# One gated-MLP stage in seven block products with its side loads reordered, in a four-layer float32 kernel on one Trainium2 core

## What is computed

```python
def first_block(...):                       # DEPTH = 2 layers
    sc = silu(c)
    for layer in range(DEPTH):
        mod = sc @ w_mod[layer] + b_mod[layer]          # 1024 x 6144 weights for one row
        shift1, scale1, gate1, shift2, scale2, gate2 = split(mod, 6)
        h = rmsnorm(x, g_attn[layer]) * (1 + scale1) + shift1
        x = x + gate1 * mixer_layer(h, w_in[layer], w_out[layer], ...)
        h = rmsnorm(x, g_mlp[layer]) * (1 + scale2) + shift2
        up = h @ w_up[layer]                             # 1024 x 5632
        u, g = up[..., :D_FF], up[..., D_FF:]            # D_FF = 2816
        g = causal_depthwise_conv(g, conv_w[layer], conv_b[layer])   # 3 taps
        x = x + gate2 * ((silu(g) * u) @ w_down[layer])

def hybrid_layer(x, ...):                   # second block, 2 layers
    mixed = concat(rms_norm(out_a), rms_norm(out_b), rms_norm(out_c))
    x = x + mixed @ w_out
    x = x + expert_choice_moe(rms_norm(x, norm_ffn), w_router, ..., w_gate, w_up, w_down)
```

## Time and profile before

| what | value |
|---|---|
| median of 3 runs | 1944.18 us (1943.29 to 1944.21) |
| the profiled execution: its own time | 1942.48 us |
| the profiled execution: span of its instructions | 1940.7 us |
| TensorE busy | 1653.6 us, 85% of the span |
| VectorE / ScalarE / GpSimd busy | 710.2 / 285.6 / 142.3 us |
| mean granted TensorE clock | 0.937 of full speed |
| data moved | 599.75 MB, mean 309 GB/s |

### The profile page before, as it was taken

How to read it: one execution, slowest core, us unless ns; L and a number is a source line. 1 busy time by engine, 2 the same in 40 slices (tenths; PEclk the granted TensorE clock), 3 DMA queues, 4 the chain that set the end, 5 groups by cost and what they waited for, 6 DMA issues and landing times.

```text
span 1940.7 us, 24600 instructions
## 1 busy us (share of the span) xinstructions
PE 1653.6 (85%) x10484; PEld 943.2 (49%) x10484; DVE 710.2 (37%) x1482; ACT 285.6 (15%) x773; POOL 142.3 (7%) x149
## 2 busy tenths in 40 slices
PE   8999999999999999999786766757999785756757
PEld 3456988544579964474432232322474432232322
DVE  1583666977628976274010010101274110010101
ACT  1243000021511001253000010001253000010000
POOL 0011000000214510310000000000220000000000
PEclk9999999999999999999897987979999898987978
DMA  9992788755235643646999999999745999999998
GB/s 354 341 338 73 249 303 299 273 196 184 88 119 185 236 151 126 192 174 259 403 429 431 427 432 426 433 429 407 252 174 238 389 430 431 425 431 427 434 428 349
DMA packets 164164, 599.75 MB, mean 309 GB/s; under 512 B 18928, under 2 KB 78064, under 8 KB 140272
## 3 DMA queue, kind: packets, MB, share of 16 engines
q1 hardware_dynamic: 163838, 598.03, 78.4%
q10 hardware_dynamic: 242, 0.53, 0.1%
HBM read 594.75 MB, written 3.80 MB: 308 GB/s over the span
## 4 chain that ended last, share of the span: by engine, by line
PE 57%; DMA 38%; DVE 3%; ACT 1%; issue 1%; POOL 0%; SPq 0%; DVEq 0%; ACTq 0%
DMA extra<-in_w_down 14%; DMA extra<-in_w_up 12%; DMA extra<-in_w_gate 11%; PE ps L1266 9%; PE ps L1379 6%; PE ps L1332 6%; PE ps L1304 5%; PE ps L1619 5%; PE ps L949 4%; PE ps L1118 4%; PE ps L1517 3%; PE ps L1216 3%; PE ps L1639 1%; DMA ring<-in_w_mod 1%; PE ps L835 1%; PE ps L857 1%
## 5 line engine op out<-in xcount | busy, mean ns | idle before, releaser
L1619 PE MATMUL ps<-ring,wide 128*32 128x256 f32 x2912 | 217.9, 465 | 120.8 <-DMA ring<-in_w_up 76.2
L1619 PEld LDWEIGHTS ps<-ring,wide 128*32 128x32 f32 x2912 | 107.3, 133 | 225.3 <-DMA ring<-in_w_up 85.8
L1639 PE MATMUL ps<-ring,wide 128*32 128x512 f32 x768 | 158.7, 641 | 45.6 <-DMA ring<-in_w_down 41.9
L3204 DVE TENSOR_TENSOR wide<-ps,wide 128x512 f32<-128x512 f32 x16 | 10.7, 670 | 508.1 <-PE ps L1619 508.1
L1266 PE MATMUL ps<-hT,ring 128*128 128x256 f32 (+1 forms) x1088 | 183.8, 330 | 0.0
L1266 PEld LDWEIGHTS ps<-hT,ring 128*128 128x128 f32 x1088 | 166.6, 191 | 17.3 <-issue 2.9
L1619 PE MATMUL ps<-extra,wide 128*32 128x256 f32 x1056 | 89.9, 512 | 62.7 <-DMA extra<-in_w_up 40.3
L1379 PE MATMUL ps<-ring,hT 128*128 128x512 f32 (+2 forms) x320 | 127.3, 555 | 0.4 <-issue 0.4
L1639 PEld LDWEIGHTS ps<-ring,wide 128*32 128x32 f32 x768 | 44.7, 117 | 155.5 <-issue 122.4
L2375 DVE SCALAR_TENSOR_TENSOR extra<-ring,sc,extra 128x512 f32<-128x512 f32 x140 | 109.8, 784 | 5.2
L1619 PEld LDWEIGHTS ps<-extra,wide 128*32 128x32 f32 x1056 | 41.9, 146 | 109.5 <-DMA extra<-in_w_up 44.2
(11 more groups left out here) (372 smaller groups left out, 2102.6 us busy)
## 6 DMA issues: line engine op xcount, KB each, us to landing
ring<-in_w_gate SPq DMA_DIRECT2D x24, 4096.0 KB, 31.4
ring<-in_w_down SPq DMA_DIRECT2D x24, 4096.0 KB, 33.7
ring<-in_w_up SPq DMA_DIRECT2D x20, 4096.0 KB, 32.6
ring<-in_w_mod SPq DMA_DIRECT2D x24, 2048.0 KB, 12.9
ring<-in_w_up SPq DMA_DIRECT2D x44, 1024.0 KB, 8.0
extra<-in_w_gate SPq DMA_DIRECT2D x8, 4096.0 KB, 35.1
extra<-in_w_up SPq DMA_DIRECT2D x8, 4096.0 KB, 33.0
ring<-in_w_in SPq DMA_DIRECT2D x13, 2048.0 KB, 13.0
```

What stands on the lines that cost most here:

```text
L1619: last = mm(ps[2 * part + e // 2][j * CAP:(j + 1) * CAP, e % 2 * 2 * P:(e % 2 + 1) * 2 * P], xsT[:, k, e * CAP:(e + 1) * CAP], expert_row( ...
L1639: last = mm(ps[6 + n][e * CAP:(e + 1) * CAP, :], hidT[:, e, k, :], expert_row(n0, e, k)[:, n * N:(n + 1) * N], start=k == 0, stop=k == KD - 1)
```

## The change

It has five parts.

1. `UP_WHOLE` becomes `(5, 2)`: layer 0's up tiles 5 to 10 are made by `up_seven` too, with all that belongs to it on GpSimd, VectorE and ScalarE.
2. The late modulations of layer 0 are moved by four tables. `FOLD_AFTER` places the tiles in the list and the folds on TensorE: 10 and 11 after the output projection (TensorE makes them after the first half of up tile 1), 12 and 13 after up tile 1, 14 and 15 after up tile 2, 16 after 3, 17 and 18 after 4, 19 after 7, 20 after 9, 21 after down tile 2. `SUM_WHOLE`, `SUM_FIRST` and `SUM_PARTS` place the sums on VectorE. The sums use three buffers in turn instead of two.
3. The convolution's first tap moves from VectorE to ScalarE in both layers, and VectorE's order of convolution, joins and row sums around a seven-product tile is another.
4. The router of the second block: rows of `w_router` are laid out in blocks, so that the load has 64-byte runs instead of 512-byte ones; its weights are multiplied by `norm_ffn` once, on GpSimd; the flipped rows are then copied by one instruction of 512 columns on each of ScalarE and VectorE instead of four scaled ones of 128.
5. `mixed_squares` runs once per attention map over four maps instead of four times in a row.

```diff
-UP_WHOLE = (11, 2)
+UP_WHOLE = (5, 2)
+FOLD_AFTER = ({("out", 1): (10, 11), ("up", 1): (12, 13), ("up", 2): (14, 15), ("up", 3): (16,), ("up", 4): (17, 18),
+               ("up", 7): (19,), ("up", 9): (20,), ("down", 2): (21,)}, {("up", 6): (0,), ("up", 7): (1,)})
+SUM_WHOLE = {0: (14,), 1: (15,), 2: (16, 17), 3: (18,)}
...
-        tiles += [(l, "out", j) for j in range(2)]
-        late = MODS[l][EARLY[l]:]
-        steps = [(l, "up", j) for j in range(UPT)] + [(l, "down", j) for j in range(NDOWN)]
-        for n, t in enumerate(steps):
+        tiles.append((l, "out", 0))
+        for t in [(l, "out", 1)] + [(l, "up", j) for j in range(UPT)] + [(l, "down", j) for j in range(NDOWN)]:
             tiles.append(t)
-            if LAGS[l] <= n < len(late) + LAGS[l]:
-                tiles.append((late[n - LAGS[l]][0], "mod", late[n - LAGS[l]][1]))
+            tiles += [(MODS[l][q][0], "mod", MODS[l][q][1]) for q in FOLD_AFTER[l].get(t[1:], ())]
...
-                                 a["w_router_2"].rearrange("l (p k) n -> p l k n", k=KD)).then_inc(sems["router_loaded"], 16)
+                                 a["w_router_2"].rearrange("l (k p) n -> p l k n", k=KD)).then_inc(sems["router_loaded"], 16)
...
                 up(1, 0, P)
                 stream_ready(2 * L + 1, 1)
+                folds(("out", 1))
                 up(0, P, P)
                 up(1, P, P)
+                folds(("up", 1))
...
-                        if j > 2:
-                            pe.wait_ge(*up_read(s, m, j - 1))
+                        if j > first:
+                            pe.wait_ge(*up_read(s, L, m, j - 1))
+                        elif m == 6 and L == 0:
+                            pe.wait_ge(*s.at("b1_mod_ready", FOLD_AFTER[0][("up", first - 1)][-1] + 1))
                         elif m == 5:
-                            pe.wait_ge(*s.at("b1_product_ready", 2))
+                            pe.wait_ge(*s.at("b1_product_ready", first - first % 2))
+                        elif m == 3:
+                            pe.wait_ge(*s.at("b1_product_ready", first - 1 + first % 2))
...
-                    for f in range(2):
-                        ts(y[:, f, :], gp[:, f, :], cc1(L, "conv_w", 2 * FCH + 2 * j + f), cc1(L, "conv_b", 2 * j + f),
-                           ALU.mult, ALU.add).then_inc(s.up(), 1)
...
+                first = UP_WHOLE[L]
+                for j in range(first - 1):
+                    conv(j)
+                    up_gated(j)
+                    if L == 0:
+                        for q in SUM_WHOLE[j]:
+                            accumulate(q)
+                up_second(first)
+                up_rows_sums()
                 if L == 0:
-                    mod_out(EARLY[L] + UPT - LAGS[L])
+                    mod_out(17)
+                    mod_out(18)
+                for j in range(first, UPT):
+                    if j in SUM_FIRST[L]:
+                        accumulate(*SUM_FIRST[L][j])
+                    conv(j - 1)
+                    up_join(j, UP_READS[:1])
+                    up_fourth(j)
+                    up_gated(j - 1)
+                    if j in SUM_PARTS[L]:
+                        accumulate(*SUM_PARTS[L][j])
...
-                    for k in range(4, 8):
-                        ts(h8[:, k, c * P:(c + 1) * P], ps[5 - 4 * c][:, (k - 4) * P:(k - 3) * P],
-                           c2(L, "norm_ffn", k), None, ALU.mult).then_inc(s.up("b2_x_by_dve" if k == 7 else None), 1)
+                    cp(h8[:, 4 - 4 * c:8 - 4 * c, c * P:(c + 1) * P], ps[5 - 5 * c][:, :].rearrange("p (k t) -> p k t", k=4))\
+                        .then_inc(s.up("b2_x_by_dve"), 1)
```

More of the change, by code:

```diff
@@ L56 @@
 EARLY = (10, 0)
-LAGS = (2, 6)
 MOD_BANK = 2
@@ L124, with _up_acts @@
 TAB = {}
+def _up_acts(l):
+    first = UP_WHOLE[l]
+    acts = [(what, j) for j in range(first - 1) for what in ("tap", "silu")]
+    for j in range(first, UPT):
+        acts += [("tap", j - 1), ("copy", j), ("silu", j - 1)]
+    return acts + [("tap", UPT - 1), ("silu", UPT - 1)]
+UP_ACTS = [_up_acts(l) for l in range(DEPTH)]
+UP_SEVEN = [UPT - UP_WHOLE[l] for l in range(DEPTH)]
 def _tab():
@@ L899, in modulation @@
                     if i // 2 in (2, 5):
-                        last = mm(ps[b][:, :], ones, acc[:, q % 2, :], start=True, stop=True)
+                        last = mm(ps[b][:, :], ones, mod_sum(L, q), start=True, stop=True)
                     else:
                         for n in range(4):
-                            last = mm(ps[b][:, n:n + 1], acc[:, q % 2, n * P:(n + 1) * P], ones[:, 0:1],
+                            last = mm(ps[b][:, n:n + 1], mod_sum(L, q)[:, n * P:(n + 1) * P], ones[:, 0:1],
                                       start=True, stop=True)
@@ L1279, in _, with folds @@
                 stream_ready(2 * L + 1, 1)
+                def folds(step):
+                    for q in FOLD_AFTER[L].get(step, ()):
+                        modulation(q)
+                folds(("out", 1))
                 up(0, P, P)
                 up(1, P, P)
-                late = len(MODS[L]) - EARLY[L]
+                folds(("up", 1))
                 def up_seven(j):
-                    pe.wait_ge(*b1_loaded(B1_AT[(1, "up", j)]))
-                    w, h = up_weights(j), in_rows()
+                    first = UP_WHOLE[L]
+                    pe.wait_ge(*b1_loaded(B1_AT[(L, "up", j)]))
+                    w, h = up_weights(L, j), in_rows()
                     s1, s2 = up_scratch(j)
@@ L1317, in _ @@
                         up(j, 0, T)
-                    if 0 <= j - LAGS[L] < late:
-                        modulation(EARLY[L] + j - LAGS[L])
+                    folds(("up", j))
                 pe.wait_ge(*s.at("b1_product_ready", UPT - 1))
@@ L1349, in _ @@
                     last.then_inc(tile_done, 1)
-                    if UPT + j - LAGS[L] < late:
-                        modulation(EARLY[L] + UPT + j - LAGS[L])
+                    folds(("down", j))
                 for j in DOWN_TAIL:
@@ L1921, in _, with up_copies @@
                     av(pT[:, j % 2, :], sm[:, j % 2, :], ACT.Silu).then_inc(s.up("b1_up_by_act"), 1)
+                def up_copies(j):
+                    act.wait_ge(*up_block(s, L, 1, j))
+                    if j >= UP_WHOLE[L] + 2:
+                        act.wait_ge(*s.at("b1_product_ready", j - 1))
+                    for c in range(2):
+                        av(up_joined(j)[:, :, 0, c * P:(c + 1) * P], ps[UP_BANK[1]][:, 0:T].rearrange("p (h t) -> p h t", h=2),
+                           ACT.Copy).then_inc(s.up("b1_up_by_act" if c else None), 1)
+                for what, j in UP_ACTS[L]:
+                    if what == "tap":
+                        tap(j)
+                    elif what == "silu":
+                        silu(j)
+                    else:
+                        up_copies(j)
                 if L == DEPTH - 1:
@@ L2089, in _ @@
                 act.wait_ge(*s.at("att_out_read", MAPS2))
-                mixed_squares((2,), pT[:, 0, :])
+                for c in range(2):
+                    mixed_squares(2, c, pT[:, 0, :])
                 act.wait_ge(*s.at("b2_out_flipped", 5))
@@ new lines, in _ @@
+                if L == 0:
+                    mod_out(17)
+                    mod_out(18)
+                for j in range(first, UPT):
+                    if j in SUM_FIRST[L]:
[6 more added lines that the diff above has]
+                        accumulate(*SUM_PARTS[L][j])
+                    if j == UPT - 1:
+                        down_sums(0)
+                    up_join(j, UP_READS[1:])
@@ L3309 @@
         rows += [i["q_norm_b_2"][l], i["k_norm_b_2"][l], i["b_router_2"][l]]
-    cols += [col(i["g_final"]), *cols1]
+    cols += [col(i["g_final"]), *cols1, *[col(i["norm_ffn_2"][l]) for l in range(DEPTH)]]
     arrays = {
```

280 lines of the change are left out of this document (146 added, 134 removed).

## The result

The changed kernel took 1971.38 us (median of 4 runs, 1968.85 to 1972.51) against 1944.2 (1943.29 to 1944.28). The ratio is 1.0138, 95% interval 1.0125 to 1.0151: 27 us slower, where 10 us slower was forecast and 17 was the upper end. The profiled execution took 1972.37 us and its span is 1970.3, so the two profiles differ by 29.6 us, somewhat more than the medians.

The account below looks back on a forecast made before the run. Layer 0's up stage was taken as bound by TensorE alone, with loads hidden. Layer 0 +10.8, clock +2.7, layer 1 -1.7, router -1.4 and squares -0.4 gave +10.0 on 1944.2, so 1954.2 us; range 1938 to 1961.

Parts of the forecast that it names:

- TensorE and VectorE against it: Layer 0's up stage, walked against load landings: three TensorE stalls of 2.9, 6.6 and 8.7 us; layer ends 10.8 us later.
- The ring's order: Layer 0's load queue, followed load by load: up tile 4 lands at 248.8, modulation 17 at 254.2, modulation 19 at 283.3.
- rival 2: Layer 0's queue: copies and router cost the ring nothing, no first or second stall, 1940.8 us; chance 0.10.
- Rival 1: Layer 0: the loads keep up, the layer gives 8.2 us, with the rest 11.7, so 1932.5 us; chance 0.14.
- The router's 3.2 us: Layer 0's load queue: the router's 2048 runs of 64 bytes take 3.2 us, bounds 0.5 and 4.
- The third wait: Layer 0, up tile 5's sixth block: waits 8.7 us for tile 4's product, behind modulation 19's first sum quarter.
- The clock: Layer 0: one clock fall behind the third stall costs 2.7 us; falls behind the first two are swallowed; bounds 0 and 5.6.
- rival 4: Layer 0: each stall drops the clock and it isn't hidden, 2 x 2.8 us more, 1960; chance 0.06.
- Rival 3: Layer 0: seven-product tiles are bound by VectorE, four tiles lose up to 5 us more, 1959; chance 0.06.
- Sum: Whole kernel: layer 0 10.8, clock 2.7, layer 1 -1.7, router -1.4 and squares -0.4 give +10.0 us.
- Layer 1: Layer 1's entry: two waits of 0.40 and 1.27 us go, -1.7 us; tiles stay bound by TensorE at 12.5.
- Second block: Second block, both layers together: router -1.4 us (bounds 0 and -2.4), squares -0.4 us (bounds 0 and -1.3).

Follow-up runs that it names:

- e1: The changed kernel with the 0.5 MB gate bias load for layer 1 issued ahead of layer 0's up tile 2 instead of 8: 1962.64 us.
- g1: The changed kernel with the gate bias load issued ahead of up tile 6 instead of 8: 1959.94 us.
- c1: The kernel before with bias_copies issued ahead of down tile 1: 1944.95 us beside 1943.42.
- e2: As e1, with the 2.7 MB of bias_copies also issued ahead of down tile 1 instead of up tile 4: 1950.88 us.
- r1: The changed kernel with the router's weights loaded in 512-byte runs as before, so other rows are chosen: 1971.49 us.
- e5: As e4, with the router's load also ahead of down tile 1 and GpSimd's two products behind layer 0's weight sums: 1944.41 us beside 1943.42.
- e3: As e2, with modulations 19 and 20 one up tile later in the list, on TensorE and on VectorE: 1942.81 us beside 1944.02.
- e4: As e3, with layer 1's fold of modulation 1 one up tile later and its tile one later in the list: 1942.99 us beside 1943.42.
- e6: As e3, with modulation 17's tile and fold behind up tile 3 instead of 4: 1943.89 us beside 1943.93.
- e7: As e6, with the sums of modulations 19 and 20 begun beside up tile 7 instead of 6, in larger pieces: 1940.13 us beside 1943.67.
- b2: The kernel before with only the second block's parts of the change (router rows, weights, one copy, squares): 1942.94 us beside 1944.02.
- e8: As e7, with the router's load ahead of down tile 1 and its GpSimd products behind the weight sums: 1939.1 us beside 1943.67.

## Why the prediction was right in its direction and wrong in its size

- **The step that failed** stands under "TensorE and VectorE against it": "VectorE waits from 240.0 to 254.2, sums to 260.3, then convolution, silu, product of tile 3 and a read of a fold to 264.0". The read of fold 16 was priced at its own 0.6 us. It needs the gate's bias, a load of its own whose issue was not moved, and the walk through the queue of loads left that load out. The read ended at 286, 22 us late; e1 and g1 show that the load's place did it. The wait at the fold of 18 was 25.9 us instead of 6.6.
- **The ring's order** was right: up tile 4 2.7 us late for 2.9, VectorE's wait for modulation 17 14.3 for 14. c1 and e2 together show that the copies are free in the old order and cost some 10 us in the new one, so rival 2 was wrong. Rival 1 falls by its own places: up tile 4 landed at 250.1 for 245.9, modulation 17 at 255.5 for 240.
- **The router's 3.2 us** were wrong as a price of packets (r1). The load as a whole costs some 2 us (e2 to e5), with 64-byte runs as with 512 (r1), so the walk had about 1 us too much for it and the wrong reason.
- **The third wait**, 8.7 us, was hidden under the second in the changed kernel and came out as 4.3 in e1 and 5.7 in e2. Its place was right, its size too large: in e1 the product of tile 4 came at 291.6 for 288.8, but TensorE came to its sixth block at 287.3 for 280.1, since the sum of 18 took 3.5 us more than the forecast had and the clock fell in tile 4 and behind the fold of 18.
- **The clock.** "After the first two it does, since the next wait is for loads and swallows it" was wrong. Tile 4, behind a wait of only 2.7 us, ran at 0.74 and took 15.5 us instead of 13.8. Behind the long wait the fall cost 2.8 us, as priced: 1.1 in the fold of 18 (1.87 us for 0.79) and 1.7 in the tiles behind it (39.20 us for three of 12.51). Another came in the down stage, 22.56 us for the 20.87 of the earlier trace rows, behind a wait of 2.0 us. The kernel before has a wait of 1.7 us there and no fall; e3, e4 and e6 have 2.0 us and no fall. So rival 4, each stall drops the clock, is in the main what happened, at 1.7 us for a fall behind a short wait.
- **Rival 3**, bound by VectorE, didn't show in the changed kernel: between its folds two tiles take 25.12 us, 12.56 each. It is what shows in e4, e5 and e7 once the loads are out of the way.
- **Sum.** The flip is 28.75 later, of that 1.2 before the stage. Forecast was 13.5. The difference of 14.1 is 19.3 more at the fold of 18, 8.7 less for the third wait, 1.7 at tile 4, 1.7 in the down stage, 0.2 less at up tile 4, and 0.1 more for the clock behind the long wait: 13.9.
- **Two slips** in the working change nothing behind them. TensorE would come to its sixth block at 279.8 and not 280.1. And rival 1's "about 56" us are about 59 by the walk's own times (185.2 to 249, less some 5 idle), which is about 460 GB/s and still more than any row shows.
- **Layer 1**: the waits at the entry went, but the fold of modulation 1 waits 1.7 us for VectorE, which it did not before, so the term of -1.7 is spent. From the flip of layer 0 to that of layer 1 it is 352.1 us against 350.7, but c1, with the code of the kernel before, takes 353.7 for it, so a term of this size can't be read from one profile.
- **Second block**: of the -1.8 forecast nothing is shown, and b2 doesn't exclude it either.

Why the best version gains 5 us and not 8 + 4 isn't settled in full. Its trace shows 0.7 us of waits for VectorE in the up tiles (1.6 in e7), the 1.7 in layer 1, and a fall of the clock in the down stage, 1.7. No run takes these away one at a time.

## What to carry to other kernels

When a consumer is moved ahead, list every load that it waits for, down to the small ones that are issued elsewhere in the queue's program; here 0.5 MB, left five tiles behind its reader, cost 8.7 us (e1), as much as the six tiles were to win (8.2). A transfer that is free today is free only in its place: before an order is changed, ask what else stands in the queue that will now be full. And look under the longest wait for those it hides: the waits came out one by one here, bias, copies, modulation 19, the slowed sum, VectorE itself, and the change paid only with 17 moved and the sums of 19 and 20 moved further (e7); the move of 17 alone (e6) gave nothing, and that of 19 and 20 without it wasn't run.

## What the runs showed of the hardware that I had not expected

- VectorE's scalar-tensor-tensor on 512 columns takes 0.76 us alone and 1.65 beside GpSimd's sums of weights. Seven of them in a modulation's sum grew from 5.5 to 9.0 us, four of the seven being the slow ones (e3). GpSimd's sums, 2.5 us a pair alone, took 2.9 and 3.4 beside them.
- A wait of 2.7 us was enough for the granted clock to show 0.74 over the next six microseconds, with 1.7 us lost. At this one place, up tile 4, the tile took 15.5 us behind a wait of 2.7 (changed kernel), 15.7 behind 2.5 (e1), 17.1 behind 3.6 (r1), and 14.1, without a fall, behind 2.4 (g1).
- In the down stage, behind a wait of 2.0 us at one and the same place, the clock fell in eight of the profiled runs (changed kernel, e1, g1, e2, e5, e7, e8, r1: 22.56 us for 48 matmuls) and not in three (e3, e4, e6: 20.87). In the three with a wait of 1.7 there (before, c1, b2) it did not fall. What decides between the eight and the three isn't shown.
- 2048 runs of 64 bytes cost no more than 256 of 512 bytes, to a few tenths of a microsecond (landings of r1 and the changed kernel), and the 128 KB cost the queue some 2 us (e2 to e5). The estimate of the prediction, scaled from the cycles that the Trainium skill gives (DMA: Bandwidth & Descriptors, "Why small descriptors are slow (HBM only)"), was 1.5 us for the 64-byte runs. No cost of the short runs was measured.
